# Summing modulation columns one block of projection work earlier in a transformer-layer kernel

## The reference, cut to what matters

```python
mod_x = (jax.nn.silu(c) @ w_mod[l] + b_mod[l])[:, None, :]
sh1, sc1, g1, sh2, sc2, g2 = jnp.split(mod_x, 6, axis=-1)
...
hx = _modulate(x, sh1, sc1)                 # needs sh1 and sc1 at once
px = hx @ w_in[l] + b_in[l]                 # the projection: 49 blocks of 128 columns
ckv_x, kr_x, cq_x, f_x, ga_x, gb_x = jnp.split(px, IN_SPLITS, axis=-1)
...                                         # attention, Fourier branch, gates
x = _layer_norm(DEEPNORM_ALPHA * x + g1 * y_x, ln1_g[l], ln1_b[l])   # g1 is needed here
y_x = _peer(_modulate(x, sh2, sc2), ...)                              # sh2, sc2 here
x = _layer_norm(DEEPNORM_ALPHA * x + g2 * y_x, ln2_g[l], ln2_b[l])   # g2 here
```

## Time and profile before

| | us |
|---|---|
| median of 3 runs | 4669.84 (4666.9 to 4673.38) |
| the profiled execution: time | 4666.9 |
| its span, first to last instruction | 4665.2 |

### The profile page before, as it was taken

The page is one execution under the profiler, slowest core; times in us unless marked ns, Lnnn a source line. Parts: engine busy times, 40 slices in busy tenths (PEclk is TensorE's granted clock), DMA queues, the critical chain, the costliest instruction groups (busy, mean ns, idle before and its releaser), DMA issues.

```text
span 4665.2 us, 56803 instructions
## 1 busy us (share of the span) xinstructions
PE 4278.6 (92%) x21163; PEld 3639.7 (78%) x21163; DVE 2940.1 (63%) x3371; ACT 1331.0 (29%) x1421; POOL 1265.7 (27%) x643
## 2 busy tenths in 40 slices
PE   7899999999988998689999999699997999999996
PEld 2588887777767876577999999698886788888885
DVE  0334775544535653554799999576675777777776
ACT  0322332333331122132233444122222222222221
POOL 0001332000001310122565443577672121221110
PEclk9899999999989999789899999899998999999998
DMA  8325775000004664266454577999996888888883
GB/s 287 107 75 157 205 216 154 17 31 31 34 32 128 190 165 112 72 153 147 123 148 139 134 177 183 329 364 347 351 361 251 303 329 321 313 311 315 317 302 133
DMA packets 698202, 917.44 MB, mean 197 GB/s; under 512 B 135467, under 2 KB 533859, under 8 KB 661987
## 3 DMA queue, kind: packets, MB, share of 16 engines
q1 hardware_dynamic: 620147, 562.95, 39.7%
q0 software_dynamic: 40928, 285.23, 16.6%
q10 hardware_dynamic: 37008, 67.65, 4.9%
HBM read 846.51 MB, written 69.22 MB: 196 GB/s over the span
## 4 chain that ended last, share of the span: by engine, by line
PE 67%; DVE 12%; DMA 11%; issue 5%; ACT 2%; SPq 1%; POOL 1%; DVEq 0%; ACTq 0%; POOLq 0%
PE ps L117 21%; PE ps L119 20%; PE ps L118 20%; DMA pu<-in_peer_u_dram 8%; DVE oneJ L1733 3%; DVE pT L1640 2%; DMA wm<-in_w_mod_dram 2%; PE ps L1916 2%; DVE ring L1755 1%; PE ps L2077 1%; DVE oneI L1734 1%; PE ps L2054 1%; PE ps L2055 0%; PE ps L2056 0%; DVE tk_pick L1708 0%
## 5 line engine op out<-in xcount | busy, mean ns | idle before, releaser
L117 PE MATMUL ps<-h2h,pTuh 128*128 128x384 f32 x2048 | 707.9, 346 | 93.5 <-POOL pTul L744 92.5
L744 POOL TENSOR_TENSOR pTul<-pT,pTuh 128x1024 fp32r<-128x1024 f32 x256 | 650.5, 2542 | 508.6 <-ACT pTuh L1098 507.1
L119 PE MATMUL ps<-h2h,pTul 128*128 128x384 f32 x2048 | 695.1, 339 | 0.0
L118 PE MATMUL ps<-h2l,pTuh 128*128 128x384 f32 x2048 | 694.9, 339 | 0.0
L117 PE MATMUL ps<-vDh,coh 128*128 128x512 f32 x1536 | 602.3, 392 | 28.8 <-DVE col L1451 28.8
L118 PE MATMUL ps<-vDl,coh 128*128 128x512 f32 x1536 | 601.6, 392 | 0.0
L119 PE MATMUL ps<-vDh,col 128*128 128x512 f32 x1536 | 601.2, 391 | 0.0
L720 POOL TENSOR_TENSOR mbuf<-mbuf,silu 128x2048 f32<-128x2048 f32 x64 | 256.1, 4002 | 1004.3 <-DMA mbuf<-in_w_mod_dram 1003.6
L1098 ACT ACTIVATE pTuh<-pT 128x1024 fp32r<-128x1024 f32 x256 | 271.8, 1062 | 845.8 <-DVE pT L1640 832.8
L117 PEld LDWEIGHTS ps<-h2h,pTuh 128*128 128x128 f32 x2048 | 392.7, 192 | 105.9 <-POOL pTul L744 90.4
L1640 DVE STREAM_TRANSPOSE pT<-pu 128x1024 f32<-128x1024 f32 x256 | 317.4, 1241 | 223.0 <-DMA pu<-in_peer_u_dram 164.7
(11 more groups left out here) (330 smaller groups left out, 7925.5 us busy)
## 6 DMA issues: line engine op xcount, KB each, us to landing
vraw<-in_peer_v_dram SPq DMA_DIRECT2D x128, 1024.0 KB
mbuf<-in_w_mod_dram SPq DMA_DIRECT2D x64, 1024.0 KB, 6.2
pu<-in_peer_u_dram ACTq DMA_DIRECT2D x256, 256.0 KB
pu<-in_peer_u_dram SPq DMA_DIRECT2D x256, 256.0 KB
wraw<-in_w_in_dram SPq DMA_DIRECT2D x48, 1024.0 KB, 8.5
wm<-in_w_mod_dram SPq DMA_DIRECT2D x16, 2048.0 KB, 8.6
gelu_scratch<-act_g SPq DMA_DIRECT2D x128, 192.0 KB
route_scratch<-route SPq DMA_DIRECT2D x24, 1024.0 KB, 5.8
```

Of the source, the lines that this page charges most:

```text
L117: pe.matmul(out, lh, rh, start=first, stop=False)
L118: pe.matmul(out, lh, rl, start=False, stop=False)
L119: return pe.matmul(out, ll, rh, start=False, stop=last)
L744: pool.tensor_tensor(pTul[s][:, c, :], pT[s][:, c, :], pTuh[s][:, c, :].bitcast(fp32), ALU.subtract).then_inc(u_lo, 1)
```

## The change

`mod_sum(j)` moves one block forward: it now stands behind block 17+j, and sum 31 behind block 48. So block 17 and block 48 are inside the loop, which has 16 turns. The sums go to PSUM bank 4 instead of 6. `mod_finish` moves on DVE from behind `queries(0)` to ahead of the first `pair_split`.

```diff
--- before.py
+++ after.py
@@ -1348,6 +1348,7 @@
             w_split(48, 0)
             mod_reduce(30, 0, 0)
             mod_reduce(31, 1, 1)
+            mod_finish(0, 2 * DC, 4)
 
 
             def pair_split(p, which):
@@ -1440,7 +1441,6 @@
             for ss in st_done:
                 dve.wait_ge(ss, 16 * ((NPX - FIRST_ST) // 2))
             queries(0)
-            mod_finish(0, 2 * DC, 6)
             attention_pair(0)
             with dve.Fori(1, HEADS // 2 - 1) as p:
                 attention_pair(p)
@@ -1994,14 +1994,11 @@
                 pe.wait_ge(mu_red, j + 1)
                 pe.matmul(pb[bank][:, bass.ds(at, 2)], mred[r][:, :], ones[:, 0:2], start=True, stop=True).then_inc(mu_sum, 1)
 
-            px_block(17, 1)
-            with pe.Fori(0, 15) as i:
+            with pe.Fori(0, 16) as i:
+                px_block(2 * i + 17, 1)
+                mod_sum(2 * i, 0, 4, 4 * i)
                 px_block(2 * i + 18, 0)
-                mod_sum(2 * i, 0, 6, 4 * i)
-                px_block(2 * i + 19, 1)
-                mod_sum(2 * i + 1, 1, 6, 4 * i + 2)
-            px_block(48, 0)
-            mod_sum(30, 0, 6, 60)
+                mod_sum(2 * i + 1, 1, 4, 4 * i + 2)
 
 
             def tile(p, n, width, parts, out_):
@@ -2111,7 +2108,6 @@
                 values(1)
 
             rope_part(0)
-            mod_sum(31, 1, 6, 62)
             pe.wait_ge(w_out_, NPX)
             query_part(0, 0)
             query_part(0, 1)
```

## The result

| | before | after |
|---|---|---|
| median, us | 4671.61 (4666.9 to 4676.85, 4 runs) | 4725.32 (4712.96 to 4730.81, 4 runs) |
| ratio of the times | | 1.0101 [1.0081, 1.0121] |
| the profiled execution, us | 4666.9, span 4665.2 | 4726.43, span 4724.8 |
| mean granted clock of PE | 0.957 | 0.952 |

The change makes the kernel 1% slower; 4731 was forecast, in a range of 4708 to 4745.

The account below looks back on a forecast made before the run. PE was taken to bound the kernel, busy 92% of the span. Stalls of 44.2 us, plus 17 for the clock, minus 0.1, gave 61 us on 4666.9, so 4728; with 2.9 for the median 4731 us, range 4708 to 4745.

Parts of the forecast that it names:

- Nothing hides a wait in this stage: Blocks 15 to 48: PE is busy for all 377.70 us, so a wait there is paid in full.
- Odd units stall, in each turn, and the chain slips with PE: Projection loop: each odd sum starts 2.18 us late, 14 times, since PE's own block ends start the chain.
- Even units don't wait: Projection loop: the even chain of 11.81 us is covered by the odd stall plus a block, so no wait.
- Starting again: After each stalled sum, PE's sequencer work shows because the queue is empty: 0.75 us per stall.
- First two units: Sums 0 and 1 at the projection loop's start, reckoned by themselves: PE 3.2 us behind.
- The clock: PE's idles in the projection loop bring 10 falls to a lower clock, 17 us in all.
- What else moves, -0.1: Sum 31, the modT write, bank 4, block 17 in the loop and SP's loads: together -0.1 us, between -0.5 and +0.3.
- Stages behind as long as before: Expected sign in the profile after: the stages after the projection keep their length.
- that the clock holds: Rival: projection stalls come, but PE's clock does not fall; 44 us, 4714, or 4708 with cheap restart; chance 0.15.
- that it falls in each turn: Rival: PE's clock falls in all 14 stalled projection turns; 68 us, 4738, or 4740 with restart at 0.87; chance 0.13.
- The fourth: Rival: attention starts at another moment, its seven pkl waits bring no clock falls; 12 us less, 4658; chance 0.03.

Follow-up runs that it names:

- experiment 6: Changed kernel with only the even sums one block early, each odd sum left behind the odd block as before: 4687.43 us, 1.0039 against the kernel before.
- experiment 4: Changed kernel with PE's loop of 16 turns written out, so no branch: 4714.44 us, 1.009 against the kernel before.
- experiment 3: Changed kernel with nine unused 512-column matmuls on PE ahead of each odd sum, to fill its wait: 4702.82 us, 1.0077.
- the first experiment: Changed kernel with sums in bank 6 and the write of modT left behind queries(0): 4720.46 us, 1.0109 against the kernel before.
- the second kernel of experiment 7: Kernel before, with each attention pair's first value rows put ahead of PE's wait for the last kTl: 4649.83 us, 0.9952.
- experiment 1's second kernel: Kernel before, with only sum 31 moved behind block 48 and the write of modT ahead of the pair splits: 4670.48 us, 0.9998.
- experiments 5: Changed kernel with identity instead of sigmoid in the stores of blocks 17 to 48, so ACT loads no table there: 4690.29 us, 1.0043.

## Why the prediction was right

Step by step, in the prediction's order:

- *Nothing hides a wait in this stage.* Right: 51.4 us more in the stage, and they reach the end.
- *Odd units stall, in each turn, and the chain slips with PE.* Right: 14 waits, the chain's steps at unchanged distances. Forecast 2.18 each, measured 2.07, 1.5 us less in all. The 0.11 is the reduce, which is shorter while PE idles (below).
- *Even units don't wait.* Right, and for the reason given: experiment 6 takes the shield away, and they wait 0.75.
- *Starting again.* The mechanism was right, the size too large: 0.75 forecast, 0.47 measured, so 6.6 us instead of 10.5. The step that failed is reading the sequencer's rows of a moment at which it ran 4 us ahead as if all of the 1.0 us were its own work; 0.4 of it was not there when the queue was empty (experiment 4). Of the 0.47, 0.35 goes with the loop's branch (experiments 4 and 6).
- *First two units.* 3.2 forecast, 2.9 measured.
- *The clock.* 10 falls forecast, 8 came, at 1.6 instead of 1.7 us each: 12.8 instead of 17. Experiment 3 shows that they come from the idle: without it none. The rule of the Trainium skill that was weighed there (TensorE: Matmul & The Clock Gate, "HAM oscillation — how this bites in real kernels"), by which a throttling wait pays in every turn, was not borne out: 8 of 14 turns paid, 7 in the first experiment, 4 in the fourth. The waits of the section's own loop are longer, 3 to 5 us by its figures, and no run here has such a loop. The attention loop, which had seemed to agree with it, paid once in seven after the second kernel of experiment 7.
- *What else moves, -0.1.* Right: experiment 1's second kernel measures 0.9998, and the wait for `pql` is unchanged.
- *Stages behind as long as before.* In this profile they are 8 us longer, by a long fall in attention's head and a little later on. The range had 5 us for such falls, the sum nothing. It offsets most of the 10 us by which the stage was over-estimated, and is why the total of 4731 looks better than its terms: they were 61 for the stage, where 51 came. That part is luck: against the median of all 18 executions, 4719.8, the forecast is 11 us too high, which is the stage's 10.

The rivals: that the clock holds was wrong (8 falls), that it falls in each turn was wrong. The fourth, a gain in attention because its waits bring no more falls, did not happen in the change, whose `pkl` waits of up to 2.0 us still bring them; but its mechanism is real: in the second kernel of experiment 7 the same waits bring one fall instead of seven, which is some 10 of its 20 us (the other 10 are the waits for `kTl`, 11.8 us).

## What to carry to other kernels

A consumer moved one step ahead is to be held against the *length of the chain* that its own engine starts, not against the mean load of the producer: DVE had 6 us to spare in every two blocks here, and PE still waited. Take the longest chain in a turn; it pays once per turn and shields the shorter ones behind it. And when the bound engine runs at full clock, look first for its short waits elsewhere: two small changes of order in the attention loop, which took 22 us of waits away, were worth 32.

## What the runs showed of the hardware

- *A fall of PE's clock does not follow from the length of one idle.* Idles of 1.95 and 1.96 us at the same place in the same loop: seven falls in seven turns before, one in seven with the turn 3 us shorter and another idle gone. Behind the 14 equal idles of 1.9 us in the changed projection loop a fall comes, from unit 5 on, behind exactly every second one; without the loop, from unit 9 on, behind every fourth. What the moment of an idle has to do with it is not shown.
- *DVE's reduce is shorter while PE idles.* The same reduce of 128 x 2048 in this stage took 3.80 to 3.83 us while PE was busy, 3.75 to 3.78 where PE idled 0.75 us at its end (experiments 5 and 6), and 3.68 to 3.70 where it idled 1.9 us. With the filler of experiment 3 PE was busy again, the reduce took 3.81 again, and the sum came 13.33 us after the block instead of 13.20.
- *A wait in a loop's last instruction costs its branch.* 0.60 us from the sum to the next block behind a stall at the end of a loop's turn, 0.24 behind a stall inside the turn (experiment 6), 0.25 without the loop, 0.13 where there is no stall.
